# The opening of a two-block transformer kernel: projections grown channel pair by channel pair, and a modulation sum moved to a later section

## The reference, cut to what matters

```python
def adaln(c, w, b):
    mod = jax.nn.silu(c) @ w + b                  # (1024) @ (1024 x 3072)
    shift, scale, gate = jnp.split(mod, 3, axis=-1)

shift, scale, gate = adaln(c, w_ada_mix[i], b_ada_mix[i])
h = rms_norm(x, norm_mix_w[i]) * (1.0 + scale) + shift
x = x + gate * mixer_sublayer(h, ...)             # proj = h @ w_in; a_half * sigmoid(b_half) -> conv ...
shift, scale, gate = adaln(c, w_ada_ffn[i], b_ada_ffn[i])
h = rms_norm(x, norm_ffn_w[i]) * (1.0 + scale) + shift
x = x + gate * ffn_sublayer(h, ...)
```

## Time and profile before

| | us |
|---|---|
| median of 3 runs (lowest to highest) | 1454.91 (1454.44 to 1455.35) |
| the profiled execution | 1460.29 |
| its span | 1458.0 |
| PE busy in the span | 1377.9 (95%) |
| DVE, ACT, POOL busy | 1013.4, 775.5, 395.3 |
| mean granted clock of TensorE | 0.979 |

### The profile page before, as it was taken

The page is one execution under the profiler, slowest core; times in us unless marked ns, Lnnn a source line. Parts: engine busy times, 40 slices in busy tenths (PEclk is TensorE's granted clock), DMA queues, the critical chain, the costliest instruction groups (busy, mean ns, idle before and its releaser), DMA issues.

```text
span 1458.0 us, 26968 instructions
## 1 busy us (share of the span) xinstructions
PE 1377.9 (95%) x10935; PEld 1339.1 (92%) x10935; DVE 1013.4 (70%) x1792; ACT 775.5 (53%) x1221; POOL 395.3 (27%) x344
## 2 busy tenths in 40 slices
PE   4899998999999999999998899999999998999997
PEld 4899997989999999999888789999998997999996
DVE  5878898857577765689476568965466566986444
ACT  3534564577364433566763446664355744766343
POOL 1047784411610000039471401750007000320000
PEclk9899999999999999999999999999999999999998
DMA  9965663323656644747310014555554311465540
GB/s 351 377 218 184 189 208 102 100 87 131 199 193 236 225 150 160 213 119 200 103 43 1 0 30 145 174 188 189 180 169 140 122 59 59 146 201 189 187 145 29
DMA packets 202488, 223.86 MB, mean 154 GB/s; under 512 B 7608, under 2 KB 197723, under 8 KB 200317
## 3 DMA queue, kind: packets, MB, share of 16 engines
q1 hardware_dynamic: 201072, 220.67, 47.0%
q10 hardware_dynamic: 1293, 1.47, 0.3%
HBM read 221.07 MB, written 1.05 MB: 152 GB/s over the span
## 4 chain that ended last, share of the span: by engine, by line
PE 74%; DVE 14%; ACT 6%; issue 3%; POOL 2%; DMA 1%; SPq 0%; ACTq 0%; DVEq 0%; POOLq 0%
PE acc L631 18%; PE acc L635 18%; PE acc L632 18%; DVE GB L2034 3%; DVE pm L2020 2%; PE acc L732 1%; DVE wlo L494 1%; DVE ADA2B L1870 1%; ACT whi L484 1%; DMA XIN<-in_x 1%; PE acc L578 1%; PE acc L579 1%; POOL AM L1346 1%; PE acc L739 1%; PE acc L585 1%
## 5 line engine op out<-in xcount | busy, mean ns | idle before, releaser
L484 ACT ACTIVATE whi<-raw 128x1024 fp32r<-128x1024 f32 (+2 forms) x380 | 381.0, 1030 | 205.9 <-PE acc L635 194.0
L494 DVE TENSOR_TENSOR wlo<-raw,whi 128x1024 fp32r<-128x1024 f32 (+2 forms) x288 | 336.6, 1197 | 160.6 <-ACT whi L484 157.6
L494 POOL TENSOR_TENSOR wlo<-raw,whi 128x1024 fp32r<-128x1024 f32 x92 | 230.3, 2523 | 753.2 <-ACT whi L484 660.5
L631 PE MATMUL acc<-HH,whi 128*128 128x256 f32 x1664 | 415.9, 287 | 2.2 <-DVE XBC L2034 2.2
L632 PE MATMUL acc<-HL,whi 128*128 128x256 f32 x1664 | 411.8, 285 | 0.0
L631 PEld LDWEIGHTS acc<-HH,whi 128*128 128x128 f32 x1664 | 319.5, 192 | 6.8 <-issue 4.3
L632 PEld LDWEIGHTS acc<-HL,whi 128*128 128x128 f32 x1664 | 319.5, 192 | 0.3 <-issue 0.2
L635 PE MATMUL acc<-HH,wlo 128*128 128x256 f32 x1664 | 234.1, 284 | 0.3 <-POOL wlo L494 0.3
L635 PEld LDWEIGHTS acc<-HH,wlo 128*128 128x128 f32 x1664 | 214.5, 190 | 0.7 <-POOL wlo L494 0.6
L631 PE MATMUL acc<-HIDH,whi 128*128 128x256 f32 x688 | 170.0, 284 | 1.9 <-issue 1.0
L632 PE MATMUL acc<-HIDL,whi 128*128 128x256 f32 x688 | 169.2, 283 | 0.0
(11 more groups left out here) (573 smaller groups left out, 2434.6 us busy)
## 6 DMA issues: line engine op xcount, KB each, us to landing
raw<-in_mlp_w SPq DMA_DIRECT2D x64, 1024.0 KB, 5.2
raw<-in_w_in SPq DMA_DIRECT2D x36, 1024.0 KB, 5.4
raw<-in_w_ffn_in SPq DMA_DIRECT2D x22, 1024.0 KB, 5.4
raw<-in_a_w_in SPq DMA_DIRECT2D x16, 1024.0 KB, 5.8
raw<-in_b_w_in SPq DMA_DIRECT2D x12, 1024.0 KB, 5.3
ADR<-in_w_ada_ffn SPq DMA_DIRECT2D x8, 1024.0 KB, 9.2
raw<-in_w_ssm_out SPq DMA_DIRECT2D x8, 1024.0 KB, 5.0
raw<-in_w_ffn_down SPq DMA_DIRECT2D x8, 768.0 KB, 4.3
```

The costliest lines, as they stand in the source:

```text
L484: act.activation(whi[:, (s.t0 + 2 * u + h) % 4, 0:k], raw[:, place(s, b, u) % 4, 0:k, h * P:h * P + P], ACT.Copy).then_inc(hi_ready, 1)
L494: v.tensor_tensor(wlo[:, slot, 0:k], raw[:, place(s, b, u) % 4, 0:k, h * P:h * P + P], whi[:, slot, 0:k].bitcast(F32), ALU.subtract).then_ ...
L631: pe.matmul(acc[:, q, 0:T], whi[:, slot, i], hh, start=first and i == 0, stop=False)
```

## The change

The weights of twelve of the 16 conv tiles (the upper half of conv_a's columns and all of conv_b's) come as eight slabs of 128 rows and 1536 columns, one for each channel tile k. Twelve PSUM sums (eight in `acc`, four in `pm`) grow over k. The modulation weights come in four groups of two channel tiles: 1024 rows by 2 x 256 columns, in two pieces of four transfers each. For a group, DVE takes eight steps of 128x512, PE four column sums, DVE makes the columns, ACT makes HH straight from H (x times the root, by POOL), DVE makes HL. POOL subtracts two thirds of each slab, DVE one third. `whi` and `wlo` hold two slabs. The remaining four tiles of conv_a follow as a section of two blocks. The FFN's modulation steps and its 16 column sums move to ssm_out, whose low halves POOL subtracts now; the masks that POOL built there move behind that.

```diff
...
-        Section("conv_a", cols(w_in, 0), 4),
+        Section("conv_a", cols(w_in, 0), 2),
         Section("xbc", cols(w_in, OFF_XBC), 12, lo="gpsimd"),
         Section("z", cols(w_in, OFF_Z), 8, lo="gpsimd"),
...
+        Section("ssm_out", a["w_ssm_out"][0], 8, (8, 8), lo="gpsimd"),
         Section("w_out", cols(a["w_out"][0], 0), 4),
         Section("ffn_in", pairs(a["w_ffn_in"][0], 0, D_FF), 22),
         Section("ffn_down", a["w_ffn_down"][0], 16, FF_CHUNKS),
...
-    ADA_FIRST = [("w_ada_mix", b) for b in range(8)]
-
-
+    FIRST = [(0, 2), (2, 2), (4, 2), (6, 2)]
+    PIECES = [(g, r0, KT // (2 if n > 1 else 1)) for g, (k0, n) in enumerate(FIRST) for r0 in range(0, KT, KT // (2 if n > 1 else 1))]
+    ENDS = [sum(1 for p in PIECES if p[0] <= g) for g in range(len(FIRST))]
+    NP = len(PIECES)
...
+    K_ORDER = (4, 5, 6, 7, 0, 1, 2, 3)
+    MIX_OK = len(FIRST) + 1
+    GATE, LATE, LAST = NP, NP + 4, NP + 12
+    MIX_LOAD = {("xbc", 4): 0, ("xbc", 6): 1, ("z", 6): 2, ("z", 7): 3}
+    LATE_LOAD = {("ssm_out", 1): (0,), ("ssm_out", 4): (1, 2), ("ssm_out", 5): (3,), ("ssm_out", 6): (4, 5),
+                 ("ssm_out", 7): (6,), ("w_out", 0): (7,)}
+    LATE_USE = {0: (0,), 1: (1, 2), 2: (3,), 3: (4, 5), 4: (6,), 5: (7,)}
...
         PRW = ar("PRW", 78, [P, 6, P])
         CIN = ar("CIN", 81, [DT, P])
...
+            def load_piece(i):
+                if i >= 4:
+                    sp.wait_ge(ada_used, i - 3)
+                g, r0, nr = PIECES[i]
+                for r in range(nr):
+                    sp.dma_start(first_piece(i)[:, r], first_src(g, r0, nr)[:, r]).then_inc(ada_in[i % 4], 16)
...
+            def load_late(i):
+                if i == 0:
+                    sp.wait_ge(u_lo, 8)
+                elif i < 3:
+                    sp.wait_ge(ylo, 16)
+                else:
+                    sp.wait_ge(ada_used, LATE + i - 2)
+                sp.dma_start(ADL[i % 3][:], late_src(i)).then_inc(ada_in[i % 3], 16)
+
+            def load_slab(i):
+                if i >= 4:
+                    sp.wait_ge(kl_p, i - 3)
+                    sp.wait_ge(kl_v, i - 3)
+                sp.dma_start(raw_slab(i), w_in[i * P:i * P + P, SLAB_C:SLAB_C + SLAB]).then_inc(landed[i % 4], 16)
+
             sp.dma_start(XIN[:], a["x"][0].rearrange("(t p) d -> p t d", p=P)).then_inc(x_in, 16)
-            for n in range(4, 7):
-                load_ada(n)
+            for g, (k0, n) in enumerate(FIRST):
+                for i in range(ENDS[g - 1] if g else 0, ENDS[g]):
+                    load_piece(i)
+                for k in range(k0, k0 + n):
+                    load_slab(k)
+            sp.dma_start(ws1[:], w_in.rearrange("(k p) c -> p k c", p=P)[:, :, OFF_DT:OFF_DT + NH]).then_inc(dt_in, 16)
             sp.dma_start(dtb[:, 0:NH], bcast(a["dt_bias"][0], NH)).then_inc(dt_in, 16)
...
                 landed_wait(act, s, b, u)
             tt = 2 * b + s.t0 + h
             act.wait_ge(w_used, tt + 1)
+            if s.name == "conv_a" and h == 0:
+                if b == 0:
+                    act.wait_ge(k_used, KT - 1)
...
+            def slab_lo(i):
+                pool.wait_ge(kh_ok, i + 1)
+                pool.tensor_tensor(slab(wlo, i)[:, SLAB_C:], raw_slab(i)[:, SLAB_C:], slab(whi, i)[:, SLAB_C:].bitcast(F32),
+                                   ALU.subtract).then_inc(kl_p, 1)
+
+            def x_scaled(k):
+                pool.tensor_tensor(H[:, k], X[:, k], NR[:, 1], ALU.mult).then_inc(xr_ok, 1)
+            pool.wait_ge(n_std, STDS["mix"])
+            for k in (0, 1):
+                x_scaled(k)
+            slab_lo(0)
+            for k in (2, 3):
+                x_scaled(k)
+            slab_lo(1)
+            for k in range(4, KT):
+                x_scaled(k)
+            for i in range(2, KT):
+                slab_lo(i)
             lo_section(SEC["xbc"])
             lo_section(SEC["z"])
             lo_section(SEC["g"])
-            pool.wait_ge(ylo, 16)
+            lo_section(SEC["ssm_out"])
+            third("ffn")
...
-                act.dma_start(PRW[p0:p0 + m, i, :], ap).then_inc(par_in, 16)
+            def rows_in(n):
+                ap, p0, i, m = pieces[n]
+                act.dma_start(PRW[p0:p0 + m, i, :], ap).then_inc(c_in if n < 3 else par_in, 16)
...
             for q in range(4):
                 act.wait_ge(xt_p, q + 1)
-                act.activation(X[:, 2 * q:2 * q + 2], acc[:, q].rearrange("p (d t) -> p d t", d=2), ACT.Copy)\
-                   .then_inc(x_ok, 1)
+                two = acc[:, q].rearrange("p (d t) -> p d t", d=2)
+                act.activation(X[:, 2 * q:2 * q + 2], two, ACT.Copy)
+                act.activation(ACC[:, 2 * q:2 * q + 2], two, ACT.Square).then_inc(n_sq, 2)
+            act.wait_ge(vchain, 2)
+            act.wait_ge(n_sum, 1)
+            inv_sqrt(act, NR[:, 1], pm[:, 1, 0:T], D, 0, n_std)
+
+            def slab_hi(i):
+                act.wait_ge(landed[i % 4], 16 * (i // 4 + 1))
+                if i >= 2:
+                    act.wait_ge(k_used, i - 1)
+                act.activation(slab(whi, i), raw_slab(i), ACT.Copy).then_inc(kh_ok, 1)
+
+            def first_hi(g, k):
+                act.wait_ge(mod_ok, g + 1)
+                act.wait_ge(xr_ok, k + 1)
+                act.activation(HH[:, k], H[:, k], ACT.Identity, scale=MOD[:, 8 + k:9 + k], bias=MOD[:, k:k + 1])\
+                   .then_inc(n_hh, 1)
 
             def small_hi(n, w_):
                 act.activation(WSH[n][:], w_[:], ACT.Copy).then_inc(wsh_ok, 1)
-
-            def conv_b_hi():
-                for h in range(2):
-                    split_hi(act, SEC["conv_b"], 0, 0, h)
-            act.wait_ge(ada_used, 1)
-            norm_act(act, "mix", mod_col(0), between=conv_b_hi)
-
-            def conv_b(b, u, h, j):
-                tile_done(act, SEC["conv_b"], b, h)
-                act.activation(G[:, ds(2 * b + h, 1)], acc[:, out_slot(SEC["conv_b"], u, h), 0:T], ACT.Sigmoid)\
-                   .then_inc(acc_free, 1)
-            def b_more(b):
-                if b == 2:
-                    act.wait_ge(dt_in, 16 * 6)
-                    small_hi(0, ws1)
-            split_section(act, split_hi, SEC["conv_b"], conv_b, extra=b_more)
+            left_rows = list(range(8, len(pieces)))
+            for g, (k0, n) in enumerate(FIRST):
+                for k in range(k0, k0 + n):
+                    slab_hi(k)
+                    first_hi(g, k)
+                    for _ in range(6 if k else 0):
+                        if left_rows:
+                            rows_in(left_rows.pop(0))
+            assert not left_rows
...
+            def first_steps(i):
+
+                g, r0, nr = PIECES[i]
+                n = FIRST[g][1]
+                v.wait_ge(ada_in[i % 4], 16 * nr_in[i])
+                dst = ADA[:, g % 2, 0:2 * n * P].rearrange("p (h c) -> p h c", h=2)
+                for r in range(nr):
+                    src, k = first_piece(i)[:, r], r0 + r
+                    if k == 0:
+                        if g > 1:
+                            v.wait_ge(ada_sum, g - 1)
+                        ins = v.tensor_scalar(dst, src, cs[:, k:k + 1], None, ALU.mult)
+                    else:
+                        ins = v.scalar_tensor_tensor(dst, src, cs[:, k:k + 1], dst, ALU.mult, ALU.add)
+                    if r < nr - 1:
+                        c.link(ins)
+                    else:
+                        ins.then_inc(ada_used, 1)
+                        v.wait_ge(ada_used, i + 1)
+            nr_in = [sum(PIECES[m][2] for m in range(i + 1) if m % 4 == i % 4) for i in range(NP)]
+
+            def slab_lo(i):
+                v.wait_ge(kh_ok, i + 1)
+                v.tensor_tensor(slab(wlo, i)[:, 0:SLAB_C], raw_slab(i)[:, 0:SLAB_C], slab(whi, i)[:, 0:SLAB_C].bitcast(F32),
+                                ALU.subtract).then_inc(kl_v, 1)
+
+            def columns_of(g):
+
+                k0, n = FIRST[g]
+                m, p_ = (ap.rearrange("p (h k) -> p h k", h=2)[:, :, k0:k0 + n] for ap in (MOD[:, 0:16], pm[:, 3, 0:16]))
+                v.wait_ge(ada_sum, g + 1)
+                c.link(v.tensor_tensor(m, p_, MODB[:, 0, :, k0:k0 + n], ALU.mult))
+                v.tensor_tensor(m, m, MODB[:, 1, :, k0:k0 + n], ALU.add).then_inc(mod_ok, 1)
+
+            for g, (k0, n) in enumerate(FIRST):
+                for i in range(ENDS[g - 1] if g else 0, ENDS[g]):
+                    first_steps(i)
+                slab_lo(k0)
+                columns_of(g)
+                for k in range(k0, k0 + n):
+                    v.wait_ge(mod_ok, g + 1)
+                    v.wait_ge(xr_ok, k + 1)
+                    v.tensor_scalar(ACC[:, k], H[:, k], MOD[:, 8 + k:9 + k], MOD[:, k:k + 1], ALU.mult, ALU.add).then_inc(n_t, 1)
+                    v.wait_ge(n_t, k + 1)
+                    v.wait_ge(n_hh, k + 1)
+                    v.tensor_tensor(HL[:, k], ACC[:, k], HH[:, k].bitcast(F32), ALU.subtract).then_inc(n_hl, 1)
```

(103 more changed lines are left out.)

294 lines of the change are left out of this document (132 added, 162 removed).

## The result

The changed kernel takes 1495.02 us (median of 4 runs, 1493.08 to 1501.16) against 1455.13 of the kernel before: ratio 1.028, 95% interval 1.025 to 1.031. That is 39.9 us slower, where 28 were forecast, and 1 us beyond the range. The profiled execution took 1493.15 us (span 1491.4), 33.4 us of span more than that of before.

A forecast was written before the change was run, and what follows sets the result against it. PE, with 74% of the chain, was taken as the bound. Opening +3 (4, less 1 for clock), ssm_out +18 and w_out +7 summed to +28: median 1483, own range 1476 to 1490, full range 1448 to 1494.

The forecast's parts named there:

- Opening, +9.5 at conv_a, less 5.3, +4 at xbc's end: Opening: conv_a ends 9.5 us later, sixteen sums leaving xbc give back 5.3, so xbc ends 4 later.
- the 1 that the forecast named as its sign: Opening: DVE's 128x512 steps averaging over 1 us would show the forecast right.
- the low products behind the sums: Opening: PE's twelve queued wlo products, 0.12 or 0.213 us each, stand behind the next sums and delay the second channel's HH.
- only move: Before `decays(0)`: PE's long wait for DVE's taps only moves with xbc's end, as the taps stay unchanged.
- ssm_out, +18: ssm_out: POOL's subtractions and DVE's steps share one port, end near 419.5 against 401.54; bounds +5.4 and +21.
- w_out, +7: Into w_out: PE stands 5.4 us for DVE's block 0 low halves, plus 1.6 of clock; bounds +4 and +8.
- No exclusion (1450): Rival 2, whole kernel: no POOL/DVE exclusion worth speaking of, xbc's end -17, ssm_out +5.4, w_out +7; 1450, chance 0.20.
- half as dear (1466): Rival 1, whole kernel: port costs half, xbc's end -6, ssm_out +11, w_out +6; 1466, chance 0.17.
- The third rival (1474): Whole kernel: xbc ends within 3 us of before, only ssm_out (+13) and w_out (+6) are paid; 1474, chance 0.12.
- Half clock throughout (1493 or above): Rival 4: half clock from 30 to 90 us and through ssm_out, +10 more; 1493 or above, chance 0.06.

The follow-up runs named there:

- Experiment 1: Changed kernel with ssm_out's low halves back on DVE, masks back ahead, late FFN loads, steps and sixteen sums left out: 1455.40 us, ratio 1.0007.
- Experiment 7: Changed kernel, in the opening PE does a group's last low-half product ahead of the next group's sums: 1495.65 us, ratio 1.0280.
- experiment 9: Kernel before, the two linked gate steps of each piece twelve taps apart (pairs took 2.6 us short, 4.6 long): 1451.94 us, ratio 0.9975.
- experiments 2 to 4: 2: changed kernel, ssm_out's low halves on DVE, 1463.05 us; 3: kernel before, those on POOL, 1475.76; 4: changed kernel without late FFN part, 1472.31.
- experiment 6: Changed kernel, POOL also subtracts w_out's block 0 behind ssm_out: 1491.20 us, ratio 1.0251.

## Why the prediction was wrong

- **Opening, +9.5 at conv_a, less 5.3, +4 at xbc's end.** Right: products from 22.96 (22), sums at 37.2, 54.7, 74.25 (38.3, 55.8, 75), twelve tiles done at 88.8 (88), conv_a's end at 105.3 (106), xbc's end +2.8. DVE's 128x512 steps averaged 1.1 to 1.2 us there, above the 1 that the forecast named as its sign. Experiment 1, without the moved sums, is at 0. One step inside was only half right: the low products behind the sums were said to hold the second HH. Experiment 7 took them away and won next to nothing; in one round ACT's own row DMAs stood in the same place.
- **The z stretch, costed at nothing.** The forecast let the long wait there "only move". Between xbc's end and ssm_out the profiled execution won back some 4 us. This is the short kind of gate pair of experiment 9, against the long kind in the profiled execution of before. The edits leave that code alone, and five of the eight traces with the new opening are long, so I take it for chance and not for a gain of the change. The changed kernel's profiled execution lies 1.9 us under its median, that of before 5.2 above its own; together they make the 7 us between the difference of the medians (39.9) and that of the profiled executions (32.9). How much of this the gate pairs explain is open.
- **ssm_out, +18.** This step failed. The exclusion of POOL and DVE was right, the path was wrong: I added up the port's work, let the last *low half* on POOL set the end, and had PE follow POOL at 4.7 us a tile. PE never waited for a low half there. From 365.4 to 404.8 it did thirteen tiles and the gates' eight sums without a wait, and POOL's last low half was done at 407.6, not 415. POOL gets in between DVE's instructions, so the late one is DVE. From PE's first readiness to ssm_out's last product it took 77.2 us instead of 48.1: +29.1, namely YL (8.1 us measured, 2 forecast), the FFN steps ahead of the sums (9.3, none forecast), the sums at the half clock (7.0, not 3.6) and products at the half clock (4.7, not 1.7). The sum of a port's work does not say which engine PE will wait for; what decides is whose result PE asks for. Also the two parts were taken as one total, while experiments 2 to 4 show them worth 0.6% (7.7 us) and 1.3 to 1.4% (some 20 us) apart and 12 to 13 us more together. Had I asked "what if only one of the two moved", the interaction would have been a term of its own.
- **w_out, +7.** The hole came as forecast, 5.4 us and the half clock behind it. Taking it away is worth less than it costs: experiment 6 likely won 3.8 us, since the wait ahead of the sums grew by 3.0.
- **Rivals.** No exclusion (1450) and half as dear (1466) are out: a YL beside a POOL subtraction took 2.6 us instead of 0.5, a step of 2.35 us took 4.4. The third rival (1474) had the opening right, xbc's end within 3 us of before, and failed by the same step as the forecast, with +13 for ssm_out. Half clock throughout (1493 or above) named nearly the right time for the wrong reason: the clock is down behind each wait and during the sums, not throughout.

## What to carry to other kernels

Before moving work from VectorE to GpSimd, count VectorE's instructions with two SBUF inputs at that place: between each two of them a GpSimd instruction that reads SBUF can get in and cost its whole length, and here the engine that ended late was VectorE. Beside VectorE's taps, with an operand in PSUM, the split cost nothing here (0.48 us a tap); putting such taps between two linked steps took PE's wait behind them away. And an idle engine in an opening is first a question of queue order: handing both channels of a pair on first, and copying the parameters later, gave 10 us here without any arithmetic less.
